# The products of the RWKV values that need no state, formed in the preparation instead of the scan

## The chip, the cores and the metric

The kernel runs on 1 core of one Trainium2 chip. The metric is the device time of one execution in microseconds, lower is better. All arithmetic of the part treated here is float32. A float32 matmul leaves two records in the trace, and each record has a weight load beside it.

## The reference, cut to what matters

The program is two blocks of a network. The second block has two mixers over 768 positions (256 of a context, 512 of the input), a gated-delta one and RWKV, and both are scanned in both directions. The change concerns RWKV alone (16 heads of 64, on 8 tiles of two heads):

```
def rwkv7_scan(r, w, k, v, kk, b_vec, s0):
    def step(state, inp):
        r_t, w_t, k_t, v_t, kk_t, b_t = inp
        sa = -jnp.einsum('bhvk,bhk->bhv', state, kk_t)
        state = (state * w_t[:, :, None, :] + sa[..., None] * b_t[:, :, None, :]
                 + v_t[..., None] * k_t[:, :, None, :])
        return state, jnp.einsum('bhvk,bhk->bhv', state, r_t)

def rwkv_mixer(u_ctx, u_lat, ...):
    ...
    for d in range(2):
        state = jnp.zeros(...)
        for i, (r, v, kk, decay, a, k_dir, z) in enumerate(streams):
            o, state = rwkv7_scan(flip_seq(r, d), ...)
            outs[i] = outs[i] + flip_seq(o, d)
            ...
```

The kernel works in 12 chunks of 64 positions. Within a chunk, with S the state at its start and V the chunk's values, the recurrence has this form, where A, R, B, K and the M are made of keys, queries and decays:

```
W  = A S + M_AK V           what the keys read
Y  = -(I + M_AB)^-1 W       the corrections
O  = R S + M_RK V + M_RB Y  the outputs (only in the 8 chunks of the input)
S' = decay * (S + B^T Y + K^T V)
```

The terms in V alone, M_AK V, M_RK V and K^T V, don't depend on S.

## The kernel before, in words

Three stages matter. Each is a block in which every engine has its own list of instructions in a fixed, written order, and the engines meet only through semaphores; a stage ends when all engines have ended.

**The preparation** (`rwkv_prep`, L3033; class `RwkvPrep`) loops over i, the 8 pairs of heads, and d, the two directions. VectorE forms the scaled keys (`operands`) and applies masks to the matrices of a chunk (`mask`); TensorE forms the matrices with `matrix` (L2955: "mb" gives M_AB and M_RB, "mk" gives M_AK and M_RK, 24 products of 64x128 into the bank ps_m) and transposes tokens with `turn_values`, `turn_b` and `turn_k` (24 products of 64x64 with the identity into the bank ps_t, all through `products`, L2915). ps_t has one user at a time: ScalarE copies each result out (`values_out`, `tokens_out`) before the next turn may start. The gates of pair i+1 (`decay_product`, `rate_product`, `norms`) lie between the products of pair i in TensorE's list, L3078 to L3104. Everything of one (i, d) lies in a buffer `ob` (three of them), and SyncE stores it with 6 DMAs (`store`, L3010) into four scratch tensors: home (decay, M_AK, A), read (R), turn (B and K by tokens) and mix (M_RB and M_RK), and with two DMAs of `store_systems` what is to be inverted. ScalarE's own queue stores the values to v_scr and the bonus. Beside all this GpSimd inverts the systems, in four batches; it does its first part during the preparation and goes on in the scan, since the stage's end stands between (L94 is the barrier).

**The scan** (`scans`, L3887) has 21 iterations n. The gated-delta scan uses n = 0 to 11, RWKV uses n = 9 to 20 (LAG = 9, step k = n - 9). RWKV starts late since its inverses come from GpSimd. SyncE loads the inverses for steps 0 to 2 at n = 7 (`load_inverse`, after GpSimd's last store) and the operands of step k+2 during step k (`load`, L3407), each transfer behind the landing of an earlier one. Of a step TensorE computes, in its list's order:

- `state_keys` (A S, 64 records) behind `value_keys` (M_AK V) in the same bank
- `state_outputs` (R S), only in steps 4 to 11
- the two stages of completing the next step's inverse (`middle`, `offdiagonal`)
- `values` (the inverse times the negated W)
- `value_outputs` (M_RK V)
- `advance`, two terms: B^T Y and K^T V, 64 records each
- `rest_outputs` (M_RB Y), then `value_keys` of the next step

All of these go through `term` (L3476 is its matmul). ScalarE and VectorE negate W, one direction each, and copy Y, one direction each. VectorE updates the state (`update`, L3602: two additions from PSUM, then the decay's product) and adds the outputs to oT (`collect`), which starts at zero. The heads' norms and gates are pipelined into the last iterations (class `HeadOutputs`).

**What follows** (`closing`) is not touched.

Of the kernel before, what the change touches and what calls it, by code (L numbers as in the profile page):

```python
# [21 lines left out]
P = 128  # L22
# [2154 lines left out]
def second(nc, k, a, hT, hc, gates_scr, p2, norms, ahead):  # L2177


    with Stage(nc, "in2") as st:  # L2180
# [11 lines left out]
        with nc.Block() as block:  # L2192
# [100 lines left out]
R_PARTS = (("home", C, R_AT + 2 * C, NCH), ("read", R_AT + 3 * C, C, T // C), ("turn", R_AT + 4 * C, 2 * C, NCH),  # L2293
           ("mix", R_AT + 6 * C, 2 * C, T // C))
# [394 lines left out]
class RwkvInputs:  # L2689
# [5 lines left out]
    def __init__(self, st, p2, norms, w_up, a_up, vectors):  # L2695
# [11 lines left out]
        self.stored, self.bonus_st, self.v_st = st.sems("r_stored", 3), st.sems("bonus_st", 2), st.sem("v_st")  # L2707
        self.system_st = st.sems("system_st", 3)

# [23 lines left out]
    def finish_small(self, eng):  # L2733
        for d in range(2):
            eng.wait_ge(self.bonus_st[d], 16 * RP // 2)
        eng.wait_ge(self.v_st, 16 * RP)


class RwkvPrep:
# [6 lines left out]
    SYSTEMS, STORED = 16 * 2, 16 * 6  # L2746

    def __init__(self, nc, st, k, given, r_scr, v_scr, bonus, systems):
        self.nc, self.k, self.given, self.r_scr, self.v_scr, self.bonus_out, self.systems = nc, k, given, r_scr, v_scr, bonus, systems
# [10 lines left out]
        self.rest = st.sb("rest", [P, GW // P])  # L2760
        self.obs = [st.sb(f"ob{u}", [P, NCH, R_COLS], at=Solver.AT + 18688 + u * 4 * NCH * R_COLS) for u in range(3)]
# [5 lines left out]
                 "bon_ps", "bon_ok", "vchain", "achain", "tick")  # L2767
# [181 lines left out]
    def turn_values(self, pe, i):  # L2949
        if i > 0:  # L2950

            pe.wait_ge(self.s["k_out"], 2 * i)
        self.products(pe, "tokv", self.v_in[i % 3], self.unit, self.ps_t, C)
# [10 lines left out]
    def turn_b(self, pe, i, d):  # L2964
        if d == 0:
            pe.wait_ge(self.s["v_out"], i + 1)
        else:
            pe.wait_ge(self.s["k_out"], 2 * i + 1)
# [6 lines left out]
    def bonus(self, pe, i):  # L2975
        if i > 0:

            pe.wait_ge(self.s["bon_ok"], i)
        self.nc.tensor.matmul(self.ps_b[:], self.k.bd64[:], self.ks[:, i % 2], start=True, stop=True).then_inc(self.s["bon_ps"], 1)

    def values_out(self, act_e, i):
        act_e.wait_ge(self.s["tokv"], i + 1)
        if i > 0:

            act_e.wait_ge(self.given.v_st, 16 * i)
        self.alink(self.nc.scalar.activation(self.vt[:], self.chunks(self.ps_t[:, 0:TA]), ACT.Copy))
        act_e.sem_inc(self.s["v_out"], 1)
        act_e.dma_start(self.v_scr[:, :, i:i + 1].rearrange("c p q v -> p (c q) v"), self.vt[:]).then_inc(self.given.v_st, 16)
# [21 lines left out]
    def store(self, sp, i, d):  # L3010

        ob, done = self.ob(i, d), self.stored[(2 * i + d) % 3]
        sp.wait_ge(self.s["k_out"], 2 * i + d + 1)
        sp.wait_ge(self.s["m_out"], 4 * i + 2 * d + 2)
        for name, col, width, n in R_PARTS:
            to = self.r_scr[name][:, d, :, i:i + 1].rearrange("c p q x -> p (c q) x")
            x = ob[:, 0:n, col:col + width]
            if name in ("home", "read"):
# [12 lines left out]


def rwkv_prep(nc, k, before, given, ahead, solver, r_scr, v_scr, bonus, systems):  # L3033


    with Stage(nc, "rprep") as st:
        m = RwkvPrep(nc, st, k, given, r_scr, v_scr, bonus, systems)
        with nc.Block() as block:
# [37 lines left out]
            def _(pe):  # L3076
                m.norms(pe, 0)
                for i in range(-1, RP):  # L3078
                    if i >= 0:
                        m.turn_values(pe, i)  # L3080
                        m.matrix(pe, i, 0, "mb")
# [6 lines left out]
                    if i >= 0:  # L3088
                        m.turn_k(pe, i, 0)
                        m.matrix(pe, i, 0, "mk")  # L3090
                    if i + 1 < RP:
                        m.decay_product(pe, i + 1, 1)
                    if i >= 0:
                        m.matrix(pe, i, 1, "mb")
                    if i + 1 < RP:
# [6 lines left out]
                    if i >= 0:  # L3102
                        m.turn_b(pe, i, 1)
                        m.turn_k(pe, i, 1)  # L3104

            @block.scalar
            def _(act_e):
                m.start_act(act_e)
                for i in range(-1, RP):
# [8 lines left out]
                    if i >= 0:  # L3118
                        m.tokens_out(act_e, i, 0, "tokk")
                    if i + 1 < RP:  # L3120
                        m.decay_gate(act_e, i + 1, 1)
                        m.rate_gate(act_e, i + 1, 1)
# [5 lines left out]
                    if i >= 0:  # L3128
                        m.tokens_out(act_e, i, 1, "tokb")
                        m.tokens_out(act_e, i, 1, "tokk")  # L3130
                        m.store_bonus(act_e, i)

# [246 lines left out]
class RwkvScan:  # L3379
# [3 lines left out]
    A_, R_, M_AK, M_RB, M_RK, B_, K_ = (("home", R_AT + C), ("read", 0), ("home", R_AT), ("mix", 0), ("mix", C), ("turn", 0), ("turn", C))  # L3383
# [3 lines left out]
    def __init__(self, nc, st, r_scr, v_scr, systems, oT, px, po):  # L3387
        self.nc, self.r_scr, self.v_scr, self.systems, self.oT = nc, r_scr, v_scr, systems, oT
# [3 lines left out]
        self.val = st.sb("rval", [P, 2, 3, RP, C], at=self.AT + 57856)  # L3392
# [12 lines left out]
        self.vlink = st.sem("rvlink")  # L3405

    def load(self, sp, k):  # L3407
# [6 lines left out]
        home, turn = self.parts["home"], self.parts["turn"]  # L3414
        at = 64 * (k // 2)
# [7 lines left out]
        sp.dma_start(self.val[:, u, 0], self.v_scr[c[0]]).then_inc(even, 16)  # L3423
        sp.dma_start(self.val[:, u, 1], self.v_scr[c[1]]).then_inc(even, 16)
        sp.wait_ge(odd, at + 32)
        sp.dma_start(self.val[64:P, u, 2], self.v_scr[c[1], 0:64]).then_inc(odd, 16)
        sp.dma_start(self.val[0:64, u, 2], self.v_scr[c[1], 64:P]).then_inc(odd, 16)
        if STEPS[k][2]:
# [3 lines left out]
            sp.wait_ge(even, at + 64)  # L3432
# [49 lines left out]
    def value_keys(self, pe, k):  # L3482

        u = k % 2
        pe.wait_ge(self.loaded[2 * u], 64 * (k // 2 + 1))
        pe.wait_ge(self.loaded[2 * u + 1], 64 * (k // 2 + 1))
        if k > 0:

            pe.wait_ge(self.s["added"], k)
        for q in range(RP):  # L3490
            for d in range(2):
                for h in range(2):
                    self.term(self.work[d], q, 1 - h if d else h, self.part(k, d, self.M_AK), self.val[:, u, d], h, True, False)

    def state_keys(self, pe, k):
# [4 lines left out]
        for q in range(RP):  # L3500
            for d in range(2):
                for h in range(2):
                    last = self.term(self.work[d], q, 1 - h if d else h, self.part(k, d, self.A_), self.state[:, d], h, False, True)
# [698 lines left out]
```

## Time and profile before

| what | value |
|---|---|
| runs | 3907.2, 3910.25, 3912.38 us; median 3910.25 |
| the profiled execution's own time | 3910.01 us |
| its span, first to last instruction | 3908.3 us |
| mean granted TensorE clock | 0.938 |
| TensorE busy over the span | 3474.3 us (89%) |
| VectorE busy | 2086.3 us (53%) |
| ScalarE busy | 665.9 us (17%) |
| GpSimd busy | 795.7 us (20%) |
| DMA, mean over the span | 156 GB/s |

Most of the 3908 us is the first block and the large projections, where TensorE is nearly full. The two stages of this case take some 840 us, from about 2850 to 3686, and can only be judged by their own stretches, not by these shares. "Busy" counts matmuls with modelled ends. PEclk is the clock that was granted to TensorE as a share of full speed. A wait is put down to what released it; "issue" is idle time in which an engine waited for nothing that the profile shows.

### The profile page before, as it was taken

Reading aid. Unit: us, or ns where it says so; the run is one execution under the profiler, and the core shown is the slowest. Engines: PE = TensorE matmul, PEld = TensorE weight load, DVE = VectorE, ACT = ScalarE, POOL = GpSimd, SP = SyncE. Lnnn points to the kernel's source line nnn. Section 1 sums busy time; section 2 is a strip of 40 time slices with the busy share of each in tenths; the row PEclk is TensorE's granted clock in tenths of the full one; section 3 lists DMA queues with packets and bytes.
Section 4 is the critical chain, followed back from the end, with each engine's and each line's share of the span. In section 5 each row is a group of like instructions: output and inputs, shape, how many; then the busy total and the mean of one; then the engine's idle time right before and its main releaser. Section 6 shows DMA issues by size and latency. Waiting matters only on the chain. (4 is left out here: it accounts for less than half of the span.)

```text
span 3908.3 us, 64427 instructions
## 1 busy us (share of the span) xinstructions
PE 3474.3 (89%) x28352; PEld 2789.0 (71%) x28352; DVE 2086.3 (53%) x2261; ACT 665.9 (17%) x1080; POOL 795.7 (20%) x817
## 2 busy tenths in 40 slices
PE   6999999999999989989999999998667765687698
PEld 3677777776787778768888888886556555576686
DVE  2477777753332646555354244336778755433564
ACT  2122222222000001121111010002233311221100
POOL 0111111111000000015003405200078769400000
PEclk8999999999999999989999999998778877898899
DMA  9444444444332445222232223244947799778443
GB/s 398 154 151 151 151 151 151 151 170 160 134 115 86 174 144 204 101 101 79 89 111 91 86 89 124 104 148 158 295 118 210 193 233 217 163 204 245 144 164 108
DMA packets 359079, 607.74 MB, mean 156 GB/s; under 512 B 136440, under 2 KB 244080, under 8 KB 330128
## 3 DMA queue, kind: packets, MB, share of 16 engines
q1 hardware_dynamic: 305488, 472.23, 38.1%
q0 software_dynamic: 21712, 92.42, 7.2%
q10 hardware_dynamic: 31600, 38.99, 2.8%
q8 instruction: 223, 3.65, 0.4%
q14 instruction: 56, 0.46, 0.0%
HBM read 469.17 MB, written 134.39 MB: 154 GB/s over the span
## 5 line engine op out<-in xcount | busy, mean ns | idle before, releaser
L182 PE MATMUL front_ps<-b_hT,p_wb 128*128 128x512 f32 x4224 | 979.4, 392 | 6.8 <-PEq L94 6.8
L182 PEld LDWEIGHTS front_ps<-b_hT,p_wb 128*128 128x128 f32 x4224 | 789.7, 188 | 187.6 <-issue 20.6
L1772 PE MATMUL in_ps<-b_hT,in_wb 128*128 128x512 f32 (+1 forms) x3264 | 750.7, 390 | 13.4 <-DVE in_wb L1759 13.4
L1772 PEld LDWEIGHTS in_ps<-b_hT,in_wb 128*128 128x128 f32 (+1 forms) x3264 | 607.0, 187 | 148.2 <-DVE in_wb L1759 13.6
L1757 DVE CAST in_wb<-in_raw 128x2048 fp32r<-128x2048 f32 (+1 forms) x68 | 82.6, 1215 | 536.4 <-PE in_ps L1772 531.5
L170 DVE CAST p_wb<-p_raw 128x2048 fp32r<-128x2048 f32 x88 | 108.0, 1227 | 430.6 <-PE front_ps L182 420.1
L813 POOL DMA_DIRECT2D front_mwb<-in_w_ada x128 | 101.4, 796 | 794.5 <-PE front_mps L823 789.3
L1772 PEld LDWEIGHTS in_ps<-b_hc,in_wb 128*128 128x128 f32 (+1 forms) x1728 | 211.4, 189 | 3.3
L1772 PE MATMUL in_ps<-b_hc,in_wb 128*128 128x256 f32 (+1 forms) x1728 | 212.6, 283 | 0.0
L172 DVE TENSOR_TENSOR p_wb<-p_raw,p_wb 128x2048 fp32r<-128x2048 f32 x88 | 201.8, 2293 | 3.0
L1211 PE MATMUL mid_ps<-mid_wb,b_hT 128*128 128x512 f32 x768 | 178.2, 393 | 13.9 <-DVE mid_wb L1196 13.9
L1081 PE MATMUL merge_ps<-b_hT,merge_wb 128*128 128x512 f32 x768 | 178.5, 395 | 12.5 <-DVE merge_wb L1069 10.1
L480 DVE SCALAR_TENSOR_TENSOR bf_both<-front_up,front_taps,bf_both 128x512 f32<-128x512 f32 x240 | 180.4, 752 | 11.8
L1211 PE MATMUL last_ps<-last_wb,last_pair 128*128 128x512 f32 x768 | 176.4, 392 | 11.1 <-DVE last_wb L1196 11.1
L1081 PEld LDWEIGHTS merge_ps<-b_hT,merge_wb 128*128 128x128 f32 x768 | 146.1, 191 | 44.9 <-DVE merge_wb L1069 10.5
L1211 PEld LDWEIGHTS mid_ps<-mid_wb,b_hT 128*128 128x128 f32 x768 | 144.6, 189 | 44.0 <-issue 14.3
L1211 PEld LDWEIGHTS last_ps<-last_wb,last_pair 128*128 128x128 f32 x768 | 145.6, 190 | 41.8 <-issue 11.4
L1759 DVE TENSOR_TENSOR in_wb<-in_raw,in_wb 128x2048 fp32r<-128x2048 f32 (+1 forms) x68 | 173.9, 2557 | 2.3
L2639 POOL TENSOR_TENSOR all_sn<-all_sn 96x62 f32<-96x62 f32 (+15 forms) x155 | 170.6, 1101 | 12.1
L2637 POOL TENSOR_TENSOR all_sn<-all_sn 96x62 f32<-96x62 f32 (+15 forms) x155 | 165.2, 1066 | 23.2 <-POOLq L94 11.1
L2007 POOL TENSOR_TENSOR in_mdx<-in_mx 128x255 f32<-128x255 f32 (+9 forms) x53 | 59.1, 1115 | 526.6 <-ACT in_mx L1984 524.4
L1790 POOL MEMSET in_gper_row<- 128x2 f32 x1 | 0.1, 100 | 679.3 <-POOLq L94 679.3
(457 smaller groups left out, 4308.6 us busy)
## 6 DMA issues: line engine op xcount, KB each, us to landing
p_raw<-in_w_in_tiles SPq DMA_DIRECT2D x88, 1024.0 KB, 6.0
in_raw<-in_w_in_tiles SPq DMA_DIRECT2D x67, 1024.0 KB, 4.8
front_mwb<-in_w_ada POOLq DMA_DIRECT2D x128, 512.0 KB, 5.0
open_wb<-in_w_ada_groups SPq DMA_DIRECT2D x32, 1024.0 KB, 11.3
g_scr<-gprep_ob SPq DMA_DIRECT2D x8, 3474.0 KB, 11.6
merge_raw<-in_w_branch_units SPq DMA_DIRECT2D x32, 512.0 KB, 4.6
mid_raw<-in_w_o_parts SPq DMA_DIRECT2D x32, 512.0 KB, 3.3
last_raw<-in_w_out_parts SPq DMA_DIRECT2D x32, 512.0 KB, 3.3
```

The costliest lines, as they stand in the source:

```text
L170: nc.vector.tensor_copy(self.wb[:, n % 2, 0], self.raw[:, n % 2]).then_inc(self.high_ok, 1)
L172: nc.vector.tensor_tensor(self.wb[:, n % 2, 1], self.raw[:, n % 2], self.wb[:, n % 2, 0].bitcast(F32), ALU.subtract).then_inc(self.w_split, 1)
L182: last = self.nc.tensor.matmul(self.ps[:, n % 2, :], self.wb[:, n % 2, x, kt, :], self.hT[:, y, kt, :], start=kt == term == 0, stop=kt == ...
L480: link(nc.vector.scalar_tensor_tensor(acc, u[:, j:j + T], self.taps[:, i, j:j + 1], acc, ALU.mult, ALU.add))
L813: pool.dma_start(self.wb[:, m % 2], w[m % 4, :, :, c:c + self.COLS]).then_inc(self.w_in[m % 2], 16)
L1081: last = self.nc.tensor.matmul(self.ps[:, u, :], self.wb[:, u, x, kt, :], self.pair[:, y, j, kt, :], start=kt == n == 0, stop=kt == self.C ...
L1211: last = self.nc.tensor.matmul(self.bank(i), self.pair[:, x, q * self.KQ + kt, t * P:(t + 1) * P], self.wb[:, n % 2, y, kt, :], start=q == ...
L1757: nc.vector.tensor_copy(high, raw).then_inc(self.high_ok, 1)
L1759: nc.vector.tensor_tensor(low, raw, high.bitcast(F32), ALU.subtract).then_inc(self.w_split, 1)
L1772: last = self.nc.tensor.matmul(self.ps[0:width, n % 3, first:end], self.wb[:, n % 2, x, kt, 0:width], h[:, y, kt, :], start=kt == term == ...
L2637: link(ops.tensor_tensor(t, y[:, :, a, j:j + 1].to_broadcast([BATCH, 2, na, ni]), y[:, :, j:j + 1, after].to_broadcast([BATCH, 2, na, ni]) ...
L2639: link(ops.tensor_tensor(y[:, :, a, after], y[:, :, a, after], t, ALU.subtract))
```

## The change

The preparation now forms the three products of V. In `RwkvPrep`, per pair i and direction d: `gains` (K^T V, 24 products of 64x64) takes the place of K's tokens in `ob`, `pulls` (M_AK V, 24 products) takes the place of M_AK, and `value_sums` (M_RK V, both directions into one bank, 32 products) goes through a new tile to a scratch tensor `sums` of 2 MB. ScalarE copies each result out; its DMA of the values is gone, one of the sums is there instead. `turn_values` of the next pair and `turn_b` of direction 1 wait for `pull_out`; `store` waits for gains and pulls and issues 7 DMAs, since turn is split into turn and gain. The first matrix of pair i+1 is issued before the gains and pulls of direction 1.

The scan has no `value_keys`, no `value_outputs` and no K term in `advance`. VectorE now negates both directions and subtracts the pulls in the same instruction, and adds the gains to the state ahead of the update. It loads half as much for turn and mix, the gains, and no values; oT is loaded with the sums at n = 9 instead of being cleared.

```
-R_PARTS = (("home", C, R_AT + 2 * C, NCH), ("read", R_AT + 3 * C, C, T // C), ("turn", R_AT + 4 * C, 2 * C, NCH),
-           ("mix", R_AT + 6 * C, 2 * C, T // C))
+R_PARTS = (("home", C, R_AT + 2 * C, NCH), ("read", R_AT + 3 * C, C, T // C), ("turn", R_AT + 4 * C, C, NCH),
+           ("gain", R_AT + 5 * C, C, NCH), ("mix", R_AT + 6 * C, C, T // C))
...
+    def gains(self, pe, i, d):
+        pe.wait_ge(self.s["k_out"], 2 * i + d + 1)
+        for c in range(NCH):
+            for h in range(2):
+                r = slice(64 * h, 64 * h + 64)
+                last = self.nc.tensor.matmul(self.ps_t[r, c * C:(c + 1) * C], self.ob(i, d)[r, c, self.TOK + C:self.TOK + 2 * C], self.vt[r, c],
+                                             start=True, stop=True)
+        last.then_inc(self.s["gain_ps"], 1)
+
+    def pulls(self, pe, i, d):
+        pe.wait_ge(self.s["gain_out"], 2 * i + d + 1)
+        pe.wait_ge(self.s["m_out"], 4 * i + 2 * d + 2)
...
+    def value_sums(self, pe, i):
+        pe.wait_ge(self.s["m_out"], 4 * i + 4)
+        pe.wait_ge(self.s["bon_ok"], i + 1)
+        for d in range(2):
+            for c in range(T // C):
+                for h in range(2):
...
     def store(self, sp, i, d):
-        sp.wait_ge(self.s["k_out"], 2 * i + d + 1)
-        sp.wait_ge(self.s["m_out"], 4 * i + 2 * d + 2)
+        sp.wait_ge(self.s["gain_out"], 2 * i + d + 1)
+        sp.wait_ge(self.s["pull_out"], 2 * i + d + 1)
...
                     if i >= 0:
                         m.turn_values(pe, i)
-                        m.matrix(pe, i, 0, "mb")
+                        if i == 0:
+                            m.matrix(pe, i, 0, "mb")
...
                         m.matrix(pe, i, 0, "mk")
+                        m.gains(pe, i, 0)
                     if i + 1 < RP:
                         m.decay_product(pe, i + 1, 1)
                     if i >= 0:
                         m.matrix(pe, i, 1, "mb")
+                        m.pulls(pe, i, 0)
...
                         m.turn_b(pe, i, 1)
                         m.turn_k(pe, i, 1)
+                        m.value_sums(pe, i)
+                        if i + 1 < RP:
+                            m.matrix(pe, i + 1, 0, "mb")
+                        m.gains(pe, i, 1)
+                        m.pulls(pe, i, 1)
...
-    def negate(self, act_e, k):
-        act_e.wait_ge(self.s["w_ok"], k + 1)
-        self.nc.scalar.activation(self.y[:, 0], self.wide(self.work[0]), ACT.Copy, scale=-1.0).then_inc(self.y_ok[0], 1)
-
-    def negate_other(self, dve, k):
+    def negate(self, dve, k):
+        u = k % 2
         dve.wait_ge(self.s["w_ok"], k + 1)
-        self.nc.vector.tensor_scalar(self.y[:, 1], self.wide(self.work[1]), -1.0, None, ALU.mult).then_inc(self.y_ok[1], 1)
+        for d in range(2):
+            pull = self.parts["home"][:, u, d, :, R_AT:R_AT + C]
+            self.nc.vector.scalar_tensor_tensor(self.y[:, d], self.wide(self.work[d]), -1.0, pull, ALU.mult, ALU.subtract).then_inc(self.y_ok[d], 1)
...
     def update(self, dve, k):
         nc, u, link, state = self.nc, k % 2, self.link, self.state
+        if STEPS[k][2]:
+            dve.wait_ge(self.s["ro_ok"], k - NCC + 1)
+        link(nc.vector.tensor_tensor(state[:], state[:], self.parts["gain"][:, u], ALU.add))
         dve.wait_ge(self.s["st_ok"], k + 1)
...
-                    if in_r(n + 1):
-                        r.value_keys(pe, n + 1 - LAG)
```

## Rows read from the trace of the kernel before

**Rows 1.** Table by stretch: start:end, length, busy (x records) per engine, PEclk, DMA, GB/s.

```profile
2893.00:2934.00 41.00, 31.79 (x460) 25.66 (x460) 32.75 (x28) 16.04 (x18) 21.60 (x21) 0.88 0.86 221
...
3056.00:3104.00 48.00, 34.63 (x474) 28.45 (x476) 39.44 (x28) 16.15 (x19) 45.49 (x33) 0.79 0.67 176
...
3380.00:3686.00 306.00, 241.25 (x7891) 207.83 (x7885) 127.55 (x165) 64.81 (x134) 13.37 (x44) 0.90 0.72 202
```

**Rows 2.** Timeline: start, length, engine, instruction, count, idle before and its releaser.

```profile
3189.91 1.20 POOL L2639 TENSOR_TENSOR all_sn<-all_sn 96x480 f32<-96x480 f32 x1
...
3202.19 1.03 POOL L2637 TENSOR_TENSOR all_sn<-all_sn 96x462 f32<-96x462 f32 x1 [11.09 <-POOLq L94]
...
3363.06 0.53 POOL L4095 DMA_DIRECT2D systems<-all_sn  x1 [0.57 <-POOL all_sn L2653]
...
3375.94 1.08 PE L3458 MATMUL scan_gpx<-scan_rinv 32*32 32x32 f32 x64 [19.97 <-DMA scan_rinv<-systems]
```

**Rows 3.** Waits of TensorE, 3376 to 3686: total us, times, longest.

```profile
PE scan_rwork L3476 <- issue: 24.3, 15, 3.0
...
PE scan_gpx L3469 <- issue: 2.3, 3, 1.1
```

**Rows 4.** DMA queues, 3376 to 3686: packets, MB, share.

```profile
q8 instruction: 63, 1.03, 1.5%
```

**Rows 5.** Groups of TensorE, 3376 to 3686: busy us, mean ns, idle before.

```profile
L3476 PE MATMUL scan_rwork<-scan_rval,scan_rops 64*64 64x64 f32 x1536 | 32.5, 235 | 8.6 <-issue 7.8 <-DVEq L3607 0.6
...
L3476 PE MATMUL scan_ro<-scan_rops,scan_rval 64*64 64x64 f32 x256 | 10.0, 233 | 0.0
```

**Rows 6.** Timeline of TensorE, one scan step.

```profile
3615.53 1.90 PE L3476 MATMUL scan_rwork<-scan_rval,scan_rops 64*64 64x64 f32 x60
...
3633.75 0.98 PE L3476 MATMUL scan_rwork<-scan_ry,scan_rops 64*64 64x64 f32 x52 [2.49 <-issue]
...
3634.58 1.52 PE L3476 MATMUL scan_rwork<-scan_rval,scan_rops 64*64 64x64 f32 x60
```

**Rows 7.** Groups of VectorE, 3376 to 3686.

```profile
L3606 DVE TENSOR_TENSOR scan_rstate<-scan_rstate,scan_rwork 128x512 f32<-128x512 f32 x24 | 16.5, 687 | 52.7 <-PE scan_rwork L3476 52.2
L3609 DVE TENSOR_TENSOR scan_rstate<-scan_rstate,scan_rops 128x1024 f32<-128x1024 f32 x12 | 14.7, 1224 | 1.8
```

**Rows 8.** Timeline of VectorE, last scan step.

```profile
3680.29 1.22 DVE L3874 TENSOR_TENSOR b2y_y2T<-b2y_y2T,b2o_late 128x1024 f32<-128x1024 f32 x1
```

**Rows 9.** Waits of SyncE's queue, 3376 to 3686.

```profile
SPq L3416 <- DVEq L3621: 18.5, 7, 5.5
```

**Rows 10.** Groups of TensorE in the preparation, 2850 to 3202.

```profile
L2921 PE MATMUL rprep_ps_m<-rprep_ob,rprep_kT 64*64 64x128 f32 x768 | 58.7, 318 | 35.9 <-issue 35.9
```

**Rows 11.** Timeline of TensorE, pair 2 of the preparation.

```profile
2941.63 2.82 PE L2921 MATMUL rprep_ps_t<-all_ident,all_x 64*64 64x64 f32 x48 [1.04 <-ACTq L2994]
...
2952.11 1.61 PE L2921 MATMUL rprep_ps_t<-all_ident,rprep_kT 64*64 64x64 f32 x48
2956.18 4.28 PE L2921 MATMUL rprep_ps_m<-rprep_ob,rprep_kT 64*64 64x128 f32 x48 [2.46 <-issue]
2960.39 1.12 PE L2912 MATMUL rprep_ps_n<-all_low,all_up 96*128 96x512 f32 x2
...
2962.41 2.84 PE L2921 MATMUL rprep_ps_m<-rprep_ob,rprep_bT 64*64 64x128 f32 x48 [0.47 <-issue]
...
2967.53 2.84 PE L2921 MATMUL rprep_ps_m<-rprep_ob,rprep_kT 64*64 64x128 f32 x48
```

**Rows 12.** Timeline of SyncE, the preparation's last transfers.

```profile
3197.89 3.04 SPq L3181 DMA_DIRECT2D all_ginv<-systems  x4
```

**Rows 13.** DMA queues, 2850 to 3202.

```profile
q1 hardware_dynamic: 118777, 53.71, 60.6%
...
q10 hardware_dynamic: 13568, 5.24, 5.9%
q8 instruction: 28, 0.46, 0.5%
```

## What the change does to the time: the prediction

> **What bounds the kernel now.** I read the table by stretch first, to see which stage is worth what. The preparation of the RWKV mixer runs from about 2850 to 3202 us, the scan stage from 3202 to 3686 us, and what follows is not touched. In no iteration of the preparation is TensorE full: 31.8 of 41 us, 34.6 of 48 [rows 1]. In the scan's second part it is busy 241 of 306 us, far above VectorE with 128 [rows 1].
>
> The timeline of the engines then says how these stages hang together. GpSimd's solver has done its part of the preparation at 3191.1 us, waits 11.09 us for the stage's end at 3202.2, and then works without a pause until it stores at 3363.06; TensorE waits 19.97 us for that data and starts the first RWKV step at 3376 [rows 2]. Two rules follow. Everything that lengthens the preparation moves the whole rest by as much, because GpSimd starts at its end. And nothing that is saved in the scan before 3376 counts; only the 12 RWKV steps from 3376 to 3686 do.
>
> Inside these 310 us I read the waits of TensorE. Besides the wait for GpSimd, nearly all idle time is "issue", time in which it waited for nothing in the profile: six lines, 33 stalls, 58.8 us together, the largest 24.3 us in 15 stalls [rows 3]. The queue table has 63 instruction packets of 16 KB in the stretch [rows 4]. A matmul here is two records with two weight loads, 7891 records with as many loads, and this divided by 63 is about 250 instructions in a packet [rows 1, 4]. A stall has its place inside a group (the last 52 of the 64 records of one group come 2.49 us late, [rows 6]), where no semaphore can be. I read this as TensorE running out of fetched instructions.
>
> At this point a rule of the Trainium skill stands against the row. "Runtime: NRT & Kernel Launch", section "Instruction fetch mechanics", says that fetches come in 16 KiB blocks of 256 instructions and are hidden, since issue is slower than the fill. The packets agree with the size, the 58.8 us of stalls do not agree with "hidden". By that rule the stalls would have another cause and stay, and the scan would give back only the work's own time.
>
> **The change, part by part.** *Scan, removed.* Three groups go: rwork from the values (the M_AK term of every step and the K term of advance, 1536 records, 32.5 us) and the values' outputs in both banks (2 x 256 records, 10.0 us for each bank [rows 5]; the banks alternate record by record, so I count 10.2 us of time). Together 2048 records and 42.7 us. Not all of it is on the path. Behind advance, TensorE runs rest_outputs and value_keys (64 records each, 1.35 us on the mean of [rows 5], 1.9 in one step of [rows 6]) while VectorE updates the state: two additions of 0.69 and one product of 1.22 us, 2.8 with the links [rows 5, 7]. TensorE's work there drops below that cover, so the M_AK half of the 32.5 us, 16 us, returns nothing. That leaves 27 us.
>
> *Scan, stalls.* The removed records are 4096 instructions, 16 packets of the 63 [rows 4, 5]. If stalls go with packets, 16/63 of 58.8 = 15 us go. Bounds: 0 if the stalls only move; and if every packet is a fixed price, 310 us / 63 = 4.9 us, 16 of them would be worth 79 us for work and stalls together. I take 15, since TensorE's stalls are 0.9 us a packet on average and the rest of the 4.9 is work.
>
> *Scan, added.* VectorE gets the addition of the gains to the state, the same shape and operands as the decay product, 1.22 us [rows 7]. In most steps it fits in VectorE's wait for advance (52.7 us idle before the 24 additions, [rows 7]), between take_other and st_ok. It doesn't in the last two steps, where VectorE goes from the outputs' additions straight into the update (1.22 us at 3680.29, then the update, [rows 8]), nor in the three steps shared with the delta scan: 5 x 1.2 = 6 us at most; I take 2.5, the last two. The two negations follow each other on VectorE (some 0.7 each, the size of an addition) instead of lying side by side; in output steps TensorE has its state outputs meanwhile, so 0 (bound: 0.7 x 12 = 8 us). The DMAs of a step get fewer by two and smaller by a quarter. SP waited only in 7 steps for a free buffer, 18.5 us in all [rows 9], so its chain of one load behind another is nearly as long as a step; as it shrinks by two landings (4 us) with the step's 3.5 us, I take 0, and up to 10 us if it becomes the limit. The 2 MB load of the sums and the memset that goes lie in stretches with nothing waiting: 0.
>
> The scan's sum: -27 - 15 + 2.5 = -40 us, about 3.3 us a step. Its ends: -25 (no stall goes: -27 + 2.5) and -77 (-79 + 2.5).
>
> *Preparation, added.* Each of the 8 pairs gets four groups of 48 records of 64x64 (gains and pulls for both directions) and one of 64. A turn of that shape takes 1.61 us, at the slow clock 2.8 [rows 11]; so 4 x 1.61 + 2.15 = 8.6 us a pair, 69 us in all, 13 a pair at the slow clock. Where it goes:
>
> (a) Between mk of direction 0 and mk of direction 1. This stretch is a chain through TensorE's ps_m and VectorE's masks, with no idle TensorE to speak of: mk0 ends at E = 2960.4, mb1 starts 2 us later, runs 2.84, and mk1 ends at E+10 [rows 11]. The gains (1.55) come before the decay product, so mb1 starts at E+3.05 instead of E+1.95: +1.1. The pulls (1.55) come before the rate product and mk1: +1.6. That is +2.7 for 7 pairs and 0.6 for the last: +19.5.
>
> (b) Between mk1 and the next mk0: value sums 2.15, gains and pulls 3.2, and two handshakes with ScalarE of 1.04 each [rows 11]: +7.4 before the values' turn (mb0 only changes places). Against it stands TensorE's idle time before mk0, 35.9 us in this group's "issue", some 5 us an iteration [rows 10], since mk0 waits for VectorE's mask of mb0. It varies (2.46 us in [rows 11]), and by the iterations I get 0, +0.8, +1.7, -0.7, +2.6, -1.0, +0.1, +2.0, together +5.5. If the clock stays low, +15 to +20.
>
> (c) The tail. The last gains and pulls come behind the last turns, with their handshakes, and the last stores wait for them; SP issues transfers until 3200.9 [rows 12] and has one DMA more per pair and direction. +4.
>
> (d) 16 more packets of instructions on the 28 of the stage [rows 13], while TensorE is less dense than in the scan: +3 (0 to 8). (e) Overlap of the last pair's terms: -2.
>
> ScalarE's five copies (0.8 us) lie in its idle time, beyond the handshakes counted. Sum: 19.5 + 5.5 + 4 + 3 - 2 = +30 us, range +20 to +50.
>
> A page's rule speaks against the stores: the Trainium skill, "DMA: Bandwidth & Descriptors", wants 512 bytes or more per transfer for the full rate, and turn, gain and mix now move 256. The count of packets stays (12288 more, 12288 fewer of the values' own); the trace has 28.7 ns a packet on the queue with mostly 512-byte ones and 24.5 on the one with mostly 256-byte ones (share x 352 us x 16 / packets, [rows 13]). By the rule and by the row the sum is the same.
>
> **The sum.** The profiled execution took 3910.0 us with a span of 3908.3, the median of the runs is 3910.25. 3910.0 + 30 - 40 gives 3900; I keep 3899, as both sums were rounded.
>
> **Rivals.** *1. The preparation grows more than the scan returns (slower).* Place: the turns' chain through ps_t before mk0. It decides once the added 7.4 us of an iteration meet less than 5 us of idle TensorE, which happens when the clock is at its low level there (granted 0.79 in the long iteration, [rows 1]): 13 us a pair, (b) becomes +25, (a) +24, with the tail +55. For it: mk0 ran at 4.28 us where mb1 had 2.84 [rows 11], a slow clock after idling. Against: a denser TensorE raises the clock. 3910 + 55 - 40 = 3925.
>
> *2. The scan is fetch-bound throughout (much faster).* Each removed packet gives 4.9 us: -77, with +30 for the preparation 3863. For it: TensorE's stalls in nearly every step. Against: VectorE's and SP's chains would take over before that.
>
> *3. The scan gives back only the removed work (no change).* The stalls find other places, because they hang on something else than the count of instructions, or SP's serial loads (18 to 20 us a step by then) and VectorE's additional 1.22 us hold the steps where TensorE doesn't. The scan then gives 27 - 2.5 = 25 us: 3910 + 30 - 25 = 3915. For it: a packet lands every 4.9 us, and TensorE could run 250 instructions in about 2.6 us (1536 records with their loads, 3072 instructions, took 32.5 us [rows 5]), so at least some packets come without a stall. Against: the stalls' place inside groups without a wait. This is what the skill's rule on instruction fetch, above, would give.
>
> **Chances.** Forecast 0.43, rival 1 0.22, rival 2 0.13, rival 3 0.22. Range 3864 to 3930; the forecast's own is 3888 to 3910. A difference of under 0.2% (7.8 us) can't be told from none here. Faster by more: 0.8 of the forecast, all of rival 2, a little of rival 3: 0.53. Slower by more: most of rival 1 and a part of 3: 0.23. Within: 0.24.
>
> **What would show it.** Right: the preparation ends near 3232 (GpSimd's restart), about 44 instruction packets in it; the stretch from mk0's end to mk1's end 12.7 us; the first RWKV step at 3406; the twelve steps in 270 us with some 47 packets and 44 us of "issue". Wrong: a preparation of over 45 us more or under 15; steps that don't shorten although 2048 records are gone; SP's wait for a free buffer gone; or VectorE waiting no longer for advance.

## The result, and the profile after

The changed kernel takes 3926.08 us (median of 9 runs, 3920.29 to 3930.76) against 3910.25 (9 runs): a ratio of 1.0036, interval 1.0025 to 1.0047. By the ratio it is slower by 14 us (by the medians 15.8); the forecast was 3899.

The profiled execution has a span of 3921.9 us. Three differences make it up: the first RWKV step starts at 3406.4 instead of 3375.9 us (+30.4), the stretch from there to the last state update takes 290.6 instead of 308.4 us (-17.8), and what follows takes 1.0 us more. 3908.3 + 30.4 - 17.8 + 1.0 = 3921.9.

The timelines show the first of them. GpSimd comes out of the stage's end 31 us later than in [rows 2], and TensorE's wait for its data ends 30 us later:

```profile
3233.52 1.02 POOL L2637 TENSOR_TENSOR all_sn<-all_sn 96x462 f32<-96x462 f32 x1 [38.69 <-POOLq L94]
...
3393.89 0.53 POOL L4145 DMA_DIRECT2D systems<-all_sn  x1 [0.57 <-POOL all_sn L2653]
...
3406.38 1.07 PE L3527 MATMUL scan_gpx<-scan_rinv 32*32 32x32 f32 x64 [24.44 <-DMA scan_rinv<-systems]
```

The preparation itself, from TensorE's first record in it to GpSimd's restart, takes 410.5 us where it was 377.6 (+32.9); it began 1.6 us earlier, and GpSimd's part behind it was 0.9 shorter.

TensorE in the preparation, pair 2 (answers to [rows 11]):

```profile
2951.56 2.06 PE L3025 MATMUL rprep_ps_b<-rprep_ob,rprep_vt 64*64 64x64 f32 x64
2960.23 5.38 PE L2925 MATMUL rprep_ps_m<-rprep_ob,rprep_bT 64*64 64x128 f32 x48 [6.61 <-DVEq L2898]
2965.37 1.75 PE L2991 MATMUL rprep_ps_t<-rprep_vt,rprep_ob 64*64 64x64 f32 x48
2968.06 1.61 PE L3002 MATMUL rprep_ps_t<-rprep_vt,rprep_ob 64*64 64x64 f32 x48 [0.94 <-ACTq L3010]
2970.72 1.61 PE L2925 MATMUL rprep_ps_t<-all_ident,all_x 64*64 64x64 f32 x48 [1.05 <-ACTq L3015]
...
2978.52 2.79 PE L2925 MATMUL rprep_ps_m<-rprep_ob,rprep_kT 64*64 64x128 f32 x48
...
2984.12 2.84 PE L2925 MATMUL rprep_ps_m<-rprep_ob,rprep_bT 64*64 64x128 f32 x48
...
2990.63 2.84 PE L2925 MATMUL rprep_ps_m<-rprep_ob,rprep_kT 64*64 64x128 f32 x48
```

See the two handshakes (0.94 and 1.05 us) ahead of the values' turn, and that the first matrix of the next pair, now ahead of gains and pulls, stands 6.61 us for VectorE's operands with all of them behind it. From mk0's end (2981.3) to mk1's end (2993.5) it is 12.2 us, where it was 10.

The two RWKV stretches of the scan in the table by stretch, first the kernel before, then the changed one (columns as in [rows 1]):

```profile
3375.94:3684.33 308.39, 244.88 (x7982) 211.36 (x7983) 126.17 (x163) 65.94 (x137) 14.59 (x48) 0.90 0.73 203
```

```profile
3406.38:3696.94 290.56, 222.42 (x5936) 190.05 (x5936) 147.63 (x187) 58.81 (x125) 14.56 (x48) 0.83 0.62 178
```

2046 records are gone. At the old clock they were 42.7 us, so 202.2 us of busy time should be left, but it is 222.4: the same work takes 20.2 us longer, at a granted clock of 0.83 instead of 0.90 (an estimate from these two clocks alone, 202.2 x 0.90 / 0.83 - 202.2, gives 17). TensorE's waits and queue of this stretch (answers to [rows 3, 4]):

```profile
PE scan_gpx L3527 <- DMA scan_rinv<-systems: 25.6, 2, 24.4
PE scan_rwork L3545 <- issue: 9.7, 5, 4.3
PE scan_rwork L3545 <- DVEq L3661: 7.7, 4, 5.5
PE scan_ro L3545 <- DMA scan_rops<-r_mix: 7.3, 3, 4.0
PE scan_gwork L3320 <- DVEq L3442: 6.3, 3, 2.8
PE scan_rwork L3545 <- DMA scan_rops<-r_gain: 4.8, 2, 2.6
```

```profile
q8 instruction: 47, 0.77, 1.1%
```

The "issue" stalls are 27 us in sum where they were 60. In their place TensorE waits for semaphores, 36.7 us without the wait for the first inverses, where it was 2.6: 13.3 for landed data (7.3 for mix, 4.8 for gains, 1.2 for later inverses), 19.2 for VectorE, and 4.2 for ScalarE and GpSimd. So of the stretch: work -42.7, clock +20.2, stalls -33.0, waits +34.1, and +3.5 of gaps that no view puts down to anything; together -17.9, which is the stretch's -17.8.

### The profile page after: what moved, and what is told of

It is laid out like the page before. It is cut to its first block and busy times, and to the rows that moved or that the text cites. A ratio compares the mean times of both kernels' runs of the same rounds, so it can differ in the third digit from the quotient of the medians.

```text
span 3921.9 us, 64548 instructions
## 1 busy us (share of the span) xinstructions
PE 3484.0 (89%) x28352; PEld 2805.3 (72%) x28352; DVE 2105.4 (54%) x2284; ACT 689.1 (18%) x1108; POOL 791.5 (20%) x817
## 5 line engine op out<-in xcount | busy, mean ns | idle before, releaser
L1772 PEld LDWEIGHTS in_ps<-b_hT,in_wb 128*128 128x128 f32 (+1 forms) x3264 | 607.2, 187 | 148.5 <-DVE in_wb L1759 13.6
L1081 PE MATMUL merge_ps<-b_hT,merge_wb 128*128 128x512 f32 x768 | 178.5, 395 | 12.5 <-DVE merge_wb L1069 10.1
L480 DVE SCALAR_TENSOR_TENSOR bf_both<-front_up,front_taps,bf_both 128x512 f32<-128x512 f32 x240 | 180.4, 752 | 11.8
L1211 PE MATMUL last_ps<-last_wb,last_pair 128*128 128x512 f32 x768 | 176.1, 392 | 11.8 <-DVE last_wb L1196 11.8
L1211 PEld LDWEIGHTS last_ps<-last_wb,last_pair 128*128 128x128 f32 x768 | 145.4, 189 | 42.4 <-issue 12.0
L2639 POOL TENSOR_TENSOR all_sn<-all_sn 96x62 f32<-96x62 f32 (+15 forms) x155 | 166.2, 1072 | 12.2
```

The source lines that it names most:

```text
L480: link(nc.vector.scalar_tensor_tensor(acc, u[:, j:j + T], self.taps[:, i, j:j + 1], acc, ALU.mult, ALU.add))
L1081: last = self.nc.tensor.matmul(self.ps[:, u, :], self.wb[:, u, x, kt, :], self.pair[:, y, j, kt, :], start=kt == n == 0, stop=kt == self.C ...
L1211: last = self.nc.tensor.matmul(self.bank(i), self.pair[:, x, q * self.KQ + kt, t * P:(t + 1) * P], self.wb[:, n % 2, y, kt, :], start=q == ...
L1772: last = self.nc.tensor.matmul(self.ps[0:width, n % 3, first:end], self.wb[:, n % 2, x, kt, 0:width], h[:, y, kt, :], start=kt == term == ...
L2639: link(ops.tensor_tensor(y[:, :, a, after], y[:, :, a, after], t, ALU.subtract))
```

## The experiments

All were timed beside the kernel before, in four groups on a chip each (medians of before 3911.3 for e1 to e4, 3907.2 for e5 to e8, 3907.6 for e9 to e12, 3910.3 for e13 and e14), so across groups ratios are what compares. The table holds each one's profiled execution: where the first RWKV step starts, the length from there to the last update, and of that stretch TensorE's busy time, records, granted clock, stalls ("issue"), and waits for semaphores without the one for the first inverses (for data in brackets). A profile shows one execution, and it isn't always the middle one: it lay 12.4 us above the median of its kernel in e5, 12.2 in e3, 10.9 in e13, 6.9 in e14, 6.5 in e7 and 5.2 in e6, 6.6 below it in e12, and within 3 us in the others. e10 has TensorE's instructions of before, and still 4.5 us more busy time at 0.87 instead of 0.90. Differences of this size between rows are not shown.

| kernel | ratio (interval) | first step | length | busy | records | clock | issue | waits (data) |
|---|---|---|---|---|---|---|---|---|
| before | 1 | 3375.9 | 308.4 | 244.9 | 7982 | 0.90 | 60.2 | 2.6 (0) |
| changed | 1.0036 (1.0025-1.0047) | 3406.4 | 290.6 | 222.4 | 5936 | 0.83 | 27.2 | 36.7 (13.3) |
| e1 | 0.9962 (0.9948-0.9975) | 3372.2 | 293.9 | 218.7 | 5936 | 0.83 | 29.7 | 40.9 (15.8) |
| e2 | 0.9987 (0.9977-0.9996) | 3376.2 | 300.2 | 237.5 | 7472 | 0.88 | 47.4 | 14.2 (9.8) |
| e3 | 1.0027 (1.0013-1.0041) | 3412.6 | 292.5 | 223.1 | 5936 | 0.84 | 30.2 | 35.8 (14.3) |
| e4 | 1.0100 (1.0086-1.0115) | 3407.5 | 312.3 | 238.0 | 7984 | 0.91 | 61.8 | 10.9 (0) |
| e5 | 1.0051 (1.0033-1.0069) | 3409.2 | 300.5 | 233.8 | 5936 | 0.79 | 42.4 | 20.0 (0) |
| e6 | 1.0000 (0.9987-1.0014) | 3385.3 | 301.8 | 235.0 | 6704 | 0.84 | 38.8 | 27.1 (12.5) |
| e7 | 0.9992 (0.9980-1.0004) | 3381.5 | 303.5 | 234.5 | 6704 | 0.84 | 50.5 | 13.8 (0.9) |
| e8 | 1.0054 (1.0035-1.0072) | 3371.5 | 327.2 | 251.1 | 7472 | 0.83 | 73.0 | 1.9 (0) |
| e9 | 1.0040 (1.0028-1.0052) | 3403.4 | 289.0 | 223.3 | 5936 | 0.83 | 27.0 | 34.3 (8.7) |
| e10 | 0.9995 (0.9984-1.0006) | 3372.3 | 309.3 | 249.4 | 7984 | 0.87 | 57.2 | 2.2 (0) |
| e11 | 1.0006 (0.9997-1.0015) | 3405.8 | 278.8 | 217.7 | 5936 | 0.85 | 29.3 | 27.2 (0) |
| e12 | 1.0033 (1.0020-1.0046) | 3386.8 | 299.2 | 231.4 | 6704 | 0.85 | 43.9 | 23.0 (9.7) |
| e13 | 1.0034 (1.0017-1.0051) | 3417.9 | 289.5 | 226.9 | 5936 | 0.81 | 37.6 | 20.3 (0) |
| e14 | 1.0054 (1.0035-1.0073) | 3407.4 | 305.1 | 242.3 | 6704 | 0.81 | 40.3 | 18.0 (0.7) |

**e1, the scan's part alone.**

```
     def gains(self, pe, i, d):
-        ...
+        pass
```

(likewise `pulls` and `value_sums`; `gains_out` and `pulls_out` only raise their semaphores, and `store` waits for `m_out` itself)

> The changed kernel without the added products in the preparation: the matmuls of gains, pulls and value_sums and ScalarE's copies of gains and pulls are left out (the stores move what lies there; the copy and the store of the sums stay). The scan is the changed one. Both theories of the scan's small gain say: the preparation goes back to about its old length, the first RWKV step to about 3378 us, and the whole from 3926 to about 3897. If the stores or the new order in TensorE's list cost something by themselves, it stays above 3905.

3895.75 us. The products and their copies cost 29 us (1.0036 - 0.9962 = 0.74%), and the scan's part alone gives 15. The preparation takes 376.2 us here, as before, though its stores are those of the changed kernel: neither the smaller packets nor the new order of what is left cost it anything. So the preparation's forecast stands and the scan's is what failed.

**e2, only the outputs' term moved.**

```
                         m.turn_k(pe, i, 1)
+                        m.value_sums(pe, i)
...
-                    if in_r(n) and STEPS[n - LAG][2]:
-                        r.value_outputs(pe, n - LAG)
```

> The kernel before with only the outputs' term moved: value_sums in the preparation, no value_outputs in the scan, mix halved, oT loaded with the sums; M_AK V and K^T V stay in the scan. The preparation gains 2.1 us of TensorE a pair in its idle time, +2 to +6. The scan loses 10.2 us of work and 4 instruction packets. Theory 1 (the clock takes back half of what TensorE is relieved of): the scan gives 5, total 3909. Theory 2 (new waits for the gains' load and VectorE's addition took it): these waits are not here, so the scan gives 10 to 14, total 3901.

3903.8 us, faster than both kernels. The preparation is as long as before (first step 3376.2), so this group does run in TensorE's idle time; the scan gives 8.2 us. It lies between the two theories: the clock fell a little (0.88), by the account above it took 2.8 of the 10.2 us of work back, and there are 9.8 us of waits for data (3.0 of them for later inverses).

**e3, no addition on VectorE.**

```
-        link(nc.vector.tensor_tensor(state[:], state[:], self.parts["gain"][:, u], ALU.add))
```

> The changed kernel without VectorE's addition of the gains to the state (12 x 1.22 us; the gains are loaded and not used). Theory 2 (VectorE's addition is late before the update in many steps): 8 to 12 us faster than the changed kernel, 3916. Theory 1: only the last two steps, 2.5 us, 3923.

3921.08 us, its interval overlaps the changed kernel's; the stretch is 292.5 us, no shorter. VectorE's addition is not where 8 to 12 us went; a few us can't be excluded.

**e4, the filler.**

```
+    def spare(self, pe, k, bank, part):
+        for q in range(RP):
+            for d in range(2):
+                for h in range(2):
+                    self.term(bank[d], q, 1 - h if d else h, part(d), self.part(k, d, self.B_), h, True, True)
```

(called once in `state_keys` and once in `advance`, in output steps twice, each ahead of the real term)

> The changed kernel with as many TensorE products in the scan as before: three groups of 64 records a step (two in context steps), on other operands and overwritten by the term behind them, at the places of the old value_keys and around advance. No loads and no VectorE work is added. Theory 1 (the clock): the granted clock of the scan's RWKV steps returns from 0.83 to 0.90, the common work gets its 20 us back, so that the 27 us of exposed work cost only about +7: 3933. Theory 2 (waits): the filler costs its exposed work and its instruction packets' stalls, +30 to +40: 3960.

3949.14 us, between the two. The clock returned to 0.91. The group "inverse times W" is the same 768 records in all three kernels (columns as in [rows 5]); before, changed, filler:

```profile
L3476 PE MATMUL scan_rwork<-scan_ry,scan_rinv 64*64 64x64 f32 x768 | 27.6, 228 | 4.9 <-issue 4.7
```

```profile
L3545 PE MATMUL scan_rwork<-scan_ry,scan_rinv 64*64 64x64 f32 x768 | 32.5, 251 | 12.4 <-issue 7.3 <-DVE scan_ry L3615 4.2 <-POOL scan_rinv L3643 0.8
```

```profile
L3545 PE MATMUL scan_rwork<-scan_ry,scan_rinv 64*64 64x64 f32 x768 | 27.0, 227 | 5.1 <-DVE scan_ry L3627 2.7 <-issue 2.4
```

The filler itself:

```profile
L3545 PE MATMUL scan_rwork<-scan_rops 64*64 64x64 f32 x2048 | 39.4, 229 | 8.9 <-issue 7.7 <-DVEq L3670 1.1 <-DVE scan_ry L3635 0.2
```

Without these 39.4 us the common work took 198.6 us, 24 less than in the changed kernel. But the stalls came back too, from 27.2 to 61.8 us for 16 packets more: 2.2 us a packet, the same as between before and changed (33.0 / 16 = 2.1). With other kernels it isn't as even: 1.9 to 3.9 us for each of the 6 packets that e6, e7, e12 and e14 have more than the changed kernel. The waits for data went. So with the whole filler all three shares of the account go back; e14 below shows that they needn't with a part of it.

**e5 and e8, the loads of a step at once.**

```
         sp.dma_start(home[:, u, 1], self.r_scr["home"][c[1], 1]).then_inc(odd, 16)
-        sp.wait_ge(even, at + 16)
         sp.dma_start(turn[:, u, 0], self.r_scr["turn"][c[0], 0]).then_inc(even, 16)
...
```

> The changed kernel; SyncE issues the loads of an RWKV step one after another without waiting for the landing of earlier ones (the waits for even, odd and first are left out of load; the wait for the free buffer and the readers' waits stay). If the new waits in the scan come from the chain of loads (TensorE waited 4.8 us for gains, 7.3 for mix, and three of the steps lasted 17.6 to 18.3 us, about the chain's length), the scan gets 6 to 12 us shorter, 3916. If they only fill what the clock and VectorE leave, or if the transfers in parallel slow each other, no difference, 3925.

> The kernel with only the outputs' term moved (3903.8 us) and its loads issued at once as well. There TensorE waited less for data, the steps are 21 us and longer: no difference, 3904. If the landing chain holds these steps too, 4 to 8 us faster, 3898.

In e5 the second answer came, no difference; e8 was outside both of its answers. The waits for data are gone (0 in both), and yet e5 takes 3927.59 us, by its interval as much as the changed kernel, and e8 3927.14, by the ratios 26 more than e2 (one run of e8, of 8706.88 us, stands apart and I can't explain it). From e2 to e8 the stretch grew by 27.0 us with the same instructions: stalls +25.6, busy time +13.6 at a clock of 0.83 instead of 0.88, waits -12.3. e5's profile shows the same signs (stalls 27 to 42, clock 0.79), but it is the slowest of its seven executions, so their size isn't shown. TensorE's largest wait in e2 and e8:

```profile
PE scan_rwork L3508 <- issue: 19.5, 10, 3.7
```

```profile
PE scan_rwork L3502 <- issue: 37.8, 16, 4.4
```

So TensorE stalls less where each load waits for the landing of an earlier one. How loads in flight delay it is not shown: an instruction packet's own transfer took 1.08 us on average in e2 and 1.09 in e8.

The traces do show that the stalls are waits for instructions, since they hold the transfer of each packet. Before, all 35 "issue" stalls of the stretch end 1.0 to 1.9 us after a packet's transfer has ended; only 22% of all TensorE's records start in this range, and none of the 4 waits for semaphores ends there. It is so for all 18 stalls of the changed kernel, all 34 of e4, all 35 of e8 and 25 of the 26 of e2. About as many packets came without a stall before and after (28 of 63 and 29 of 47): nearly all that the change took away were ones that had stalled TensorE.

**e6 and e7, K^T V or M_AK V back in the scan.** e6 takes `gains` and `gains_out` out of the preparation and puts the K term of `advance` and its values' load back; e7 does so with `pulls`, `value_keys` and the old negations.

> The changed kernel with K^T V back in the scan (768 records, 6 packets, as in the kernel before, with its values loaded) and without the gains' products and copies in the preparation; M_AK V and the sums stay moved. The preparation gets 13 us shorter. In the scan 16 us of work and, at the 2.1 us of stall that a packet was worth between the two kernels, 12 us of stalls come back, less what the clock gives back (5 to 8) and less than 4 of waits: +17. Together 3930; if the clock gives nothing, 3938.

> The changed kernel with M_AK V back in the scan (value_keys behind rest_outputs, 768 records, 6 packets) and without the pulls' products and copies in the preparation; K^T V and the sums stay moved. The preparation gets 13 us shorter. The work lies beside VectorE's update, so only stalls come back, up to 12 us, less 5 for the clock: 3926 - 13 + 7 = 3920. If value_keys is wholly hidden, 3913.

3906.45 and 3907.13 us, both the same as before, and both better than expected. In the scan e6 lost less than expected (+11.2 us against the changed kernel's stretch, for +17) and e7 more (+12.9, for +7); what made both fast is the preparation. There one group with its handshake moves the first step by 9.4 (pulls) or 5.6 us (gains), the two together by 30.4. The prediction's two places differ in this. In (a), from mk0's end to mk1's end over all pairs, the costs add up: +13.1 with the pulls, +8.2 with the gains, +22.0 with both. In (b), from mk1's mask to the next mk0's, they don't: -4.6 and -10.2 singly, +7.9 together. That one group with its handshake finds room in the idle time of (b) and the second doesn't fits these numbers; no run isolates it.

In the scan the second term brings nothing beyond e2 (301.8 and 303.5 us against 300.2), only the third does (290.6). The profiles say where the second went: from e2 to e6 768 records with some 16 us of work are gone, but TensorE's busy time fell by 2.5 us only, as the clock went from 0.88 to 0.84, and the waits rose by 12.9 while the stalls fell by 8.6. In e7 the busy time fell by 3.0.

**e9 and e12, the matrix in its old place.**

```
                         m.turn_values(pe, i)
-                        if i == 0:
-                            m.matrix(pe, i, 0, "mb")
+                        m.matrix(pe, i, 0, "mb")
...
                         m.value_sums(pe, i)
-                        if i + 1 < RP:
-                            m.matrix(pe, i + 1, 0, "mb")
```

> The changed kernel with the first matrix of pair i+1 issued where it was before, behind turn_values(i+1), and not ahead of gains and pulls of direction 1. In the changed kernel TensorE waits 27.6 us in 6 stalls at this matrix for VectorE's operands (10.2 at most), with gains, pulls and the turn queued behind it. If this wait is what makes the preparation 30 us longer, the products run in the idle time and 10 to 18 us come back: 3912. If the handshakes of the products themselves are the cost (7.4 us against 5 us of idle time), it gives at most 3 us, 3924.

> The kernel with the sums and M_AK V moved and K^T V in the scan (3906.5 us), with the first matrix of pair i+1 in its old place. Its preparation was 9 us longer than before, with one group and one handshake more ahead of the turn. If the matrix' place is the cost there too, the preparation gets 6 to 9 us shorter and the whole 3899; else 3905.

e9: 3921.09 us, first step 3 us earlier: the small answer. e12: 3919.11 us, outside both of its answers and 0.3% slower than e6, with the first step 1.5 us later; its profile is the fastest of its five executions (span 3910.8) and doesn't show the rest. The hoisted matrix was not the fault, in spite of its 27.6 us of waits.

**e10, the kernel before with few value loads; e11, the changed one with few gain loads.**

```
+        if k < 2:
             sp.dma_start(gain[:, u, 0], self.r_scr["gain"][c[0], 0]).then_inc(even, 16)
...
+        else:
+            sp.sem_inc(even, 16)
+            sp.sem_inc(odd, 16)
```

> The kernel before; from RWKV step 2 on the values are not loaded (11 of 13 MB of value loads a run are left out, TensorE reads what lies there). TensorE's list has as many instructions as before. If its issue stalls hang on the number of instruction packets alone, they stay at 60 us and the kernel at 3908. If a packet is late because it shares the DMA engines with data, they fall by a third and the scan by 10 to 20 us: 3893.

> The changed kernel; from RWKV step 2 on the gains are not loaded. It relieves SyncE's chain by two landings (some 4 us a step) and the DMA engines by 5 MB. If the waits for landed operands (13 us in the scan) cost what they show, 8 to 13 us faster, 3915. If the clock or the issue stalls take it, no more than 3, 3923.

e10: 3906.82 us, no difference; the stalls stay at 57 us with less data, so they hang on the count of packets (and, by e8, on bursts), not on the mean load. e11: 3911.86 us, 0.3% below the changed kernel, as the theory of waits said: the stretch is 278.8 us, no wait for data is left, and SyncE stands longer before a free buffer. It takes away two landings of a step and 5 MB of traffic at once; e13 tries the landings alone. Its wait in the changed kernel and in e11:

```profile
SPq L3487 <- DVEq L3674: 30.0, 5, 9.8
```

```profile
SPq L3487 <- DVEq L3678: 54.7, 9, 13.2
```

**e13, gains in one transfer with turn.** (`R_PARTS` has turn with 2 * C columns and no gain; direction 1's gains reach the scan with the two heads exchanged.)

> The changed kernel with the gains stored and loaded in one transfer with turn (128 columns, 512 bytes a packet, 6 DMAs a store again) and not as a tensor of their own. The bytes are the same, SyncE's chain has one landing less per direction and step (a turn took 2.7 us and a gain 3.5 to land; one of double size took 4.4 in the kernel before). If the number of landings in the chain is the cost, the scan gets 4 to 8 us shorter: 3919. If the bytes are, nothing: 3925.

3923.18 us, not to be told from the changed kernel. The waits for data went to 0, and the stretch is 289.5 us, no shorter: in this one profile the stalls rose to 37.6 and the clock fell to 0.81. So a shorter chain alone gave nothing back, and neither did loads without a chain (e5); only e11, without the gains' loads, did. Whether the waits for data cost what they show stays open.

**e14, a third of the filler.** (Only the call in `state_keys`.)

> The changed kernel with a third of the filler: one group of 64 overwritten TensorE products a step, at the place of the old value_keys, beside VectorE's update (768 records, 6 packets). With the whole filler the clock went from 0.83 to 0.91 and the common work lost 27 us. If the clock follows the amount of TensorE's work, it comes to about 0.86 and the common work loses 8 us, while the stalls grow by 12: +8, 3934. If the filler around advance did it, the clock stays at 0.83 and the kernel takes 3940.

3935.68 us with a clock of 0.81. The total fits the first answer (3934) and the clock is as low as the second one has it, or lower. So the clock doesn't simply follow the amount; one group beside VectorE's update didn't raise it.

## Why the prediction was wrong

- **The preparation, +30: right, in its working only in part.** First step +30.4 us, GpSimd's restart at 3233.5 (forecast 3232), 44 instruction packets as forecast. (a) came to 12.2 instead of 10 us in six pairs and 7.8 more in one, 22.0 in all for 19.5. (b), from mk1's mask to the next mk0's, came to +7.9 for 5.5, but from -7.6 to +8.8 in the single iterations, where I had -1.0 to +2.6: its sum is partly luck. (c), from the last mask to GpSimd's restart, came to +2.6 for 4. TensorE's clock rose from 0.81 to 0.88 over the preparation (0.96 in four of the stretches), so rival 1's condition, a low clock, did not occur, though its total of 3925 was hit.
- **The scan, -40: the step that failed.** It gave 17.8. Two costs were left out or too small, the clock (0, measured 20.2) and TensorE's waits for other engines and for data (16 of cover and 2.5, measured 34.1), and one gain was too small, the stalls (15, measured 33.0). The misses partly cancel, or the scan would have given next to nothing.
- **The clock had no term at all.** I priced the kept work at the old clock. It cost 20.2 us, and e4 shows that it is the clock and not the new order, since the same records are fast again beside the filler. The other kernels with these 5936 records were granted 0.79 to 0.85, those with 7982 or 7984 0.87 to 0.91.
- **"I take 0" for SyncE's chain failed.** 13.3 us of waits for data came. The chain doesn't shrink by two landings: `load` has six waits for landings in an output step, as before. By the transfers it did get shorter, from 24.2 to 18.8 us (first issue to last landing, mean of the eight output steps), but four of the steps it had to keep up with now took only 18 to 20 us. Such waits are in rival 3, whose 3915 is nearer than my 3899, but its other half, stalls that find other places, did not occur. How much the waits cost stays open: e11 gives the stretch 11.8 us back, e5 and e13 have none of them and give nothing.
- **"I take 15" for the stalls was too small: 33.0.** e4's filler brought them back at the same price, 2.1 to 2.2 us a packet. I spread the 58.8 us over all 63 packets; 28 of them had come without a stall, and the removed ones were mostly the others.
- **The removed work was right in size (42.7 us).** Its cover by VectorE's update shows as a wait of 7.7 us where I took 16.
- **VectorE's addition, +2.5: small, as said** (e3).
- **The two rules.** Of the Trainium skill's "Runtime: NRT & Kernel Launch", section "Instruction fetch mechanics", the block size agrees with the rows, "hidden" doesn't: stalls of 27 to 73 us end behind a packet's transfer and move with the number of packets and the bursts of loads. By the rule the scan would have kept its 60 us of stalls; it lost 33. On the rule of 512 bytes in the Trainium skill's "DMA: Bandwidth & Descriptors", section "Specifications": the store queue of the preparation took 23.3 ns a packet at 345 bytes mean (54.3% of 382 us x 16 over 142496 packets) where it was 28.7 at 452 [rows 13]. So smaller packets were cheaper each and 6% dearer by the byte (0.067 and 0.063 ns), which leans the rule's way. The count of packets did not stay, as I had said: the two queues have 144800 where they had 132345, mostly since the gains are 24576 packets and the values were 12288. e1, with the same stores, shows that none of this cost time.

What stays open: what decides the clock inside the scan (e4 raised it and e14 didn't; in e5, e10 and e13 it was lower without any change of TensorE's work, in one execution each), e12's median beside its profile, how loads in flight lengthen the stalls, and why the waits for data bring time back only when the loads themselves go.

## What to carry to other kernels

Before work is taken off the busiest engine, ask what else runs close behind it: here a chain of loads of 16 to 23 us stood behind output steps of 18 to 28. Price the work that stays at a lower clock as well; here the clock took back 20.2 of 42.7 us, and 2.8 of 10.2 in e2. Move the term that needs no handshake and fits in idle time (e2), and count moved terms together, since two that cost 5.6 and 9.4 us singly cost 30 together. And look whether the profile is a typical execution before you read a few us from it.

## What the runs showed that I had not expected

Transfers issued at once made the kernel slower, by 26 us (e8 against e2), mostly through TensorE's own instruction stalls: 73.0 instead of 47.4 us, although no data came late. And an equal list of 768 records took 27.6, 32.5 and 27.0 us in three kernels that differ in what stands around it.
